# The input norm's root applied at the bank, and x split on arrival

## The reference, cut to what matters

```python
def rmsnorm(x, g):
    xf = x.astype(F32)
    y = xf * lax.rsqrt(jnp.mean(xf * xf, -1, keepdims=True) + EPS)
    return (y * g.astype(F32)).astype(x.dtype)

def mamba_layer(x, ...):
    h = rmsnorm(x, norm_g)
    proj = h @ w_in                  # z (4096), x/B/C (6144), dt (64)
    z, xbc, dt_raw = ...
    xbc, conv_new = causal_conv(xbc, conv_prev, conv_w, conv_b)   # per channel, 4 taps, silu
    dt = softplus(dt_raw + dt_bias)
    ...                              # recurrence over chunks, per head
    return x + y @ w_out, conv_new, s
```

## Time and profile before

| | us |
|---|---|
| median of 3 runs | 2285.92 |
| lowest, highest | 2285.22, 2286.48 |
| the profiled execution | 2281.53 |
| its span, first to last instruction | 2279.7 |
| TensorE busy | 2182.0 (96%) |
| VectorE busy | 1345.5 (59%) |
| ScalarE busy | 1109.9 (49%) |
| GpSimd busy | 1078.4 (47%) |

### The profile page before, as it was taken

One profiled execution on the slowest core, in us unless ns is written; L12 is line 12 of the kernel. 1 busy time (PEld: TensorE's weight loads), 2 busy tenths in 40 slices (PEclk: granted clock), 3 DMA queues, 4 the chain that ended last, 5 costly groups with the idle time before them and its releaser, 6 DMA issues. The chain is left out here.

```text
span 2279.7 us, 37485 instructions
## 1 busy us (share of the span) xinstructions
PE 2182.0 (96%) x13846; PEld 1868.0 (82%) x13846; DVE 1345.5 (59%) x2193; ACT 1109.9 (49%) x2824; POOL 1078.4 (47%) x712
## 2 busy tenths in 40 slices
PE   6999999999999999899998995999999999999799
PEld 5998888898998989598997773787787877877599
DVE  4766676767676767754214766665565665665510
ACT  4455454545545455553344544554554545545332
POOL 5665656565656655256672003533333333333166
PEclk9999999999999999899999997999999999999899
DMA  4564646564656465343443322212022122021544
GB/s 160 201 215 174 216 171 213 182 216 168 221 171 213 175 211 199 145 141 130 168 166 139 113 86 88 65 30 70 27 72 63 32 63 73 22 74 31 227 155 147
DMA packets 80623, 309.69 MB, mean 136 GB/s; under 512 B 14610, under 2 KB 22162, under 8 KB 54978
## 3 DMA queue, kind: packets, MB, share of 16 engines
q1 hardware_dynamic: 80450, 307.41, 39.1%
HBM read 279.72 MB, written 27.66 MB: 135 GB/s over the span
## 5 line engine op out<-in xcount | busy, mean ns | idle before, releaser
L691 POOL TENSOR_TENSOR w_lo<-raw,w_hi 128x1024 fp32r<-128x1024 f32 x218 | 540.2, 2499 | 367.9 <-ACT w_hi L903 367.8
L110 PE MATMUL bank<-h_hi,w_hi 128*128 128x304 f32 (+1 forms) x1520 | 471.7, 310 | 11.7 <-DVE h_lo L322 6.2
L112 PE MATMUL bank<-h_hi,w_lo 128*128 128x304 f32 (+1 forms) x1520 | 458.3, 302 | 0.0
L111 PE MATMUL bank<-h_lo,w_hi 128*128 128x304 f32 (+1 forms) x1520 | 456.5, 300 | 0.0
L903 ACT ACTIVATE w_hi<-raw 128x1024 fp32r<-128x1024 f32 x216 | 216.6, 1050 | 343.1 <-PE bank L112 334.8
L110 PE MATMUL bank<-b_hi,a_hi 128*128 128x512 f32 x896 | 357.7, 399 | 16.1 <-POOL a_lo L2442 8.5
L111 PE MATMUL bank<-b_lo,a_hi 128*128 128x512 f32 x896 | 350.8, 392 | 0.0
L112 PE MATMUL bank<-b_hi,a_lo 128*128 128x512 f32 x896 | 350.7, 391 | 0.0
L110 PEld LDWEIGHTS bank<-h_hi,w_hi 128*128 128x128 f32 x1520 | 286.1, 188 | 27.6 <-DVE h_lo L322 8.1
L111 PEld LDWEIGHTS bank<-h_lo,w_hi 128*128 128x128 f32 x1520 | 286.9, 189 | 2.3 <-issue 1.7
L112 PEld LDWEIGHTS bank<-h_hi,w_lo 128*128 128x128 f32 x1520 | 286.4, 188 | 0.0
(11 more groups left out here) (386 smaller groups left out, 4275.4 us busy)
## 6 DMA issues: line engine op xcount, KB each, us to landing
raw<-in_a_units SPq DMA_DIRECT2D x112, 1024.0 KB, 4.9
raw<-in_b_in_units SPq DMA_DIRECT2D x20, 1024.0 KB, 4.7
past<-in_cache SPq DMA_DIRECT2D x64, 288.0 KB, 3.2
pt<-in_cache_t SPq DMA_DIRECT2D x64, 256.0 KB, 2.5
raw<-in_o_units SPq DMA_DIRECT2D x16, 1024.0 KB, 5.2
s_in<-in_state_in SPq DMA_DIRECT2D x31, 512.0 KB, 7.0
out_state_out<-s_in SPq DMA_DIRECT2D x31, 512.0 KB, 6.9
s_t<-in_state_t SPq DMA_DIRECT2D x15, 1024.0 KB, 6.5
```

The lines of the kernel that those rows point to most:

```text
L110: nc.tensor.matmul(out, a[0], b[0], start=start, stop=False)
L111: nc.tensor.matmul(out, a[0], b[1], start=False, stop=False)
L112: return nc.tensor.matmul(out, a[1], b[0], start=False, stop=stop)
L691: nc.gpsimd.tensor_tensor(w_lo[u % 2][:, c], raw[u % 2][:, c], w_hi[u % 2][:, c].bitcast(F32), ALU.subtract).then_inc(lo_done, 1)
```

## The change

1. `load_stage` and `root_stage` are gone; a class `Entry` does their work inside `mamba_stage`. x arrives in quarters between the two halves of unit 0; `norms` goes out second; unit 1, `narrow`, `ones`, `eps` and ten small loads follow on the same queue.
2. x * norm (without the root) is split as it arrives: ScalarE makes the high part with norm as scale, VectorE the low part with one instruction. VectorE also makes the low parts of units 0 and 1, which GpSimd made, and clears the six buffers that GpSimd cleared.
3. The squares come behind the splits on ScalarE, into four free buffers; VectorE adds them up in five instructions, and one product by ones (halfway in the dt projection) gives the sum. ScalarE makes the root behind the split of unit 2.
4. The root is applied as a block leaves its bank: `evac` moves from ScalarE to VectorE and multiplies by `rs`. The old conv columns stay with ScalarE (`conv_past`), with a semaphore of their own. The dt rows are multiplied too (`rooted`).
5. In group 0 VectorE's order has the copies between the convs, `sums` and the copies of the turned rows (now `turned_back`) are apart, and ScalarE runs `ends` right behind `softplus`. From group 1 on, VectorE's copy of a block stands ahead of `heads` of the next iteration, and that of the tenth ahead of the first `add_out`.

The buffer `tmp` now shares its place with `y_lo`. The core of the diff:

```diff
     put("d_skip", [P, GROUPS, PAIRS])
     put("gate_norm", [P, GROUPS, PAIRS])
-    put("dt_bias", [HEADS, 1])
-    put("a_log", [HEADS, 1])
+    put("dt_in", [HEADS, 2])
+    put("rs", [P, TOK])
...
-def load_stage(nc, ctx, m, d):
...
-def root_stage(nc, ctx, m, psum, first, x_src, loads):
...
-class Scaled:
...
+class Entry:
+    SQUARES = ("gate0", "gate1", "y", "scratch")
...
+    def load(self, sp):
+        m, d = self.m, self.d
+
+        def x(n):
+            sp.dma_start(m["x"][:, 4 * n:4 * n + 4, :], d["x"][:, 4 * n:4 * n + 4, :]).then_inc(self.x_in[n], 16)
+
+        def first(n):
+            sp.dma_start(m["raw0"][:, HALVES[n]], d["a_units"][0][:, HALVES[n]]).then_inc(self.first_in[n], 16)
+        x(0)
+        sp.dma_start(m["norms"][:], d["norms"]).then_inc(self.gains_in, 16)
+        first(0)
+        x(1)
+        first(1)
+        x(2)
+        x(3)
+        sp.dma_start(m["raw1"][:], d["a_units"][1]).then_inc(self.second_in, 16)
+        sp.dma_start(m["narrow"][:], d["narrow"]).then_inc(self.narrow_in, 16)
+        for name in ("ones", "eps"):
+            sp.dma_start(m[name][:], d[name]).then_inc(self.ones_in, 16)
+        for dst, src in self.small:
+            sp.dma_start(dst, src).then_inc(self.small_in, 16)
+
+    def on_scalar(self, act):
+        nc, m = self.nc, self.m
+
+        def high(k):
+            if k % 4 == 0:
+                act.wait_ge(self.x_in[k // 4], 16)
+            nc.scalar.activation(m["h_hi"][:, k, :], m["x"][:, k, :], ACT.Copy, scale=self.gain(k)).then_inc(self.high_done, 1)
+
+        def first(n):
+            act.wait_ge(self.first_in[n], 16)
+            nc.scalar.activation(m["w_hi0"][:, HALVES[n]], m["raw0"][:, HALVES[n]], ACT.Copy).then_inc(self.first_high, 1)
+        nc.scalar.preload_act_table_set("natural_log_exp_and_others")
+        act.wait_ge(self.gains_in, 16)
         for k in range(KT):
+            high(k)
+            if k in (3, 7):
+                first(k // 4)
+        act.wait_ge(self.second_in, 16)
+        for c in HALVES:
+            nc.scalar.activation(m["w_hi1"][:, c], m["raw1"][:, c], ACT.Copy).then_inc(self.second_high, 1)
+
+    def squares(self, act):
         for k in range(KT):
+            self.nc.scalar.activation(self.m[self.SQUARES[k // 4]][:, k % 4, :], self.m["x"][:, k, :], ACT.Square).then_inc(self.squared, 1)
+
+    def root(self, act):
+        rs = self.m["rs"][:]
+        act.wait_ge(self.ones_in, 32)
+        act.wait_ge(self.summed, 1)
+        self.nc.scalar.activation(rs, self.SUM[:, 0:TOK], ACT.Ln, bias=self.m["eps"][:, 0:1], scale=1.0 / D_MODEL).then_inc(self.rooted, 1)
+        act.wait_ge(self.rooted, 1)
+        self.nc.scalar.activation(rs, rs, ACT.Exp, scale=-0.5).then_inc(self.rooted, 1)
+
+    def on_vector(self, dve, lo_done):
+        nc, m = self.nc, self.m
+        for name in ("dec0", "dec1", "cb", "c_diag", "cbuf0", "cbuf1"):
+            nc.vector.memset(m[name][:], 0.0)
+
+        def low(k):
+            dve.wait_ge(self.high_done, k + 1)
+            nc.vector.scalar_tensor_tensor(m["h_lo"][:, k, :], m["x"][:, k, :], self.gain(k), m["h_hi"][:, k, :].bitcast(F32),
+                                           op0=ALU.mult, op1=ALU.subtract).then_inc(self.low_done, 1)
+
+        def unit_low(u, n, high):
+            c = HALVES[n]
+            dve.wait_ge(high, n + 1)
+            return nc.vector.tensor_tensor(m[f"w_lo{u}"][:, c], m[f"raw{u}"][:, c], m[f"w_hi{u}"][:, c].bitcast(F32), ALU.subtract)
+        for k in range(KT):
+            low(k)
+            if k in (3, 7):
+                unit_low(0, k // 4, self.first_high).then_inc(self.first_low, 1)
+        for n in range(2):
+            unit_low(1, n, self.second_high).then_inc(lo_done, 1)
+
+    def add(self, dve):
+        nc, sq = self.nc, [self.m[n] for n in self.SQUARES]
+        v = Chain(dve, self.added)
+        for n in (1, 2, 3):
+            dve.wait_ge(self.squared, 4 * n + 4)
+            v(nc.vector.tensor_tensor(sq[0][:], sq[0][:], sq[n][:, 0:4, :], ALU.add))
+        v(nc.vector.tensor_tensor(sq[0][:, 0:2, :], sq[0][:, 0:2, :], sq[0][:, 2:4, :], ALU.add))
+        v(nc.vector.tensor_tensor(sq[0][:, 0, :], sq[0][:, 0, :], sq[0][:, 1, :], ALU.add))
+
+    def sum(self, pe):
+        pe.wait_ge(self.ones_in, 32)
+        pe.wait_ge(self.added, 5)
+        self.nc.tensor.matmul(self.SUM[:, 0:TOK], self.m["ones"][:], self.m["gate0"][:, 0, :], start=True, stop=True).then_inc(self.summed, 1)
 
...
-    def high(self, act):
+    def high(self, act, narrow_in):
+        act.wait_ge(narrow_in, 16)
         self.nc.scalar.activation(self.w_hi[:, 0:self.N], self.m["narrow"][:, 0:self.N], ACT.Copy).then_inc(self.split, 1)
-        self.nc.scalar.activation(self.seq_a, self.m["a_log"][:, 0:1], ACT.Exp).then_inc(self.a_step, 1)
+
+    def rates(self, act):
+        self.nc.scalar.activation(self.seq_a, self.m["dt_in"][:, 1:2], ACT.Exp).then_inc(self.a_step, 1)
+
+    def rooted(self, dve):
+        dve.wait_ge(self.proj, 1)
+        self.nc.vector.tensor_tensor(self.xb, self.P0[0:HEADS, 0:TOK], self.m["rs"][0:HEADS, :], ALU.mult).then_inc(self.scaled, 1)
 
     def softplus(self, act):
         nc, ab = self.nc, self.ab
-        act.wait_ge(self.proj, 1)
-        nc.scalar.activation(self.xb, self.P0[0:HEADS, 0:TOK], ACT.Identity, bias=self.m["dt_bias"][:, 0:1]).then_inc(self.a_step, 1)
+        act.wait_ge(self.scaled, 1)
+        nc.scalar.activation(self.xb, self.xb, ACT.Identity, bias=self.m["dt_in"][:, 0:1]).then_inc(self.a_step, 1)
...
+    def turned_back(self, dve):
+        nc = self.nc
...
-    def project(self, pe):
+    def project(self, pe, halfway):
         pe.wait_ge(self.split, 2)
         for k in range(KT):
+            if k == KT // 2:
+                halfway(pe)
...
-                if u >= 3:
+                if u == 2:
+                    sp.wait_ge(entry.first_low, 2)
+                else:
                     sp.wait_ge(lo_done, 2 * (u - 2))
...
+            entry.load(sp)
             unit(2)
...
-            scaled_x.on_pool(pool)
-            for u in range(1, LAST_UNIT + 2):
+            pool.wait_ge(lo_done, 2)
+            for u in range(2, LAST_UNIT + 2):
                 for n, c in enumerate(HALVES):
-                    if u == 1:
-                        first.high_done(pool, 1, n)
-                    else:
-                        pool.wait_ge(hi_done, 2 * (u - 2) + n + 1)
+                    pool.wait_ge(hi_done, 2 * (u - 2) + n + 1)
...
+                else:
+                    pe.wait_ge(entry.first_low, half + 1)
...
-                        scaled_x.low_done(pe, j)
+                        pe.wait_ge(entry.low_done, j + 1)
...
-                        steps.project(pe)
+                        steps.project(pe, entry.sum)
                     elif k == 3:
+                        entry.small_wait(pe)
                         steps.turn(pe)
...
-            def evac(kind, g, k):
...
+            def conv_past(kind, g, k):
+                if kind != "c":
+                    return
+                conv_saved.wait(act, g if k >= 2 else g - 1, k - 2 if k >= 2 else CONV_BLK - 2 + k)
+                if k == 0:
+                    act.wait_ge(co_in[g % 2], 16 * (g // 2 + 1))
+                nc.scalar.activation(by_seq(cbuf[k % 2], 7)[:, :, 0:3], conv_old[g % 2][:, k], ACT.Copy).then_inc(old_done.sem, 1)
...
-            scaled_x.on_scalar(act)
-            first.high(act, 1)
-            steps.high(act)
+            entry.on_scalar(act)
+            steps.high(act, entry.narrow_in)
+            entry.squares(act)
+            entry.small_wait(act)
+            steps.rates(act)
             for g in range(GROUPS):
                 u = unit_at(g)
                 first_in = IN_UNITS if g else CONV_BLK
                 of_g = blocks[at["z" if g else "c", g, 0]:][0:IN_UNITS]
                 for k in range(first_in):
                     split(u + k + 1)
+                    if g == 0 and k == 1:
+                        entry.root(act)
                     if k:
-                        evac(*of_g[k - 1])
+                        conv_past(*of_g[k - 1])
                     if g == 0 and k == 2:
                         steps.softplus(act)
-                    if g == 0 and k == 3:
                         steps.ends(act)
                     if k == 0 and g == 1:
-                        evac("z", 0, PAIRS - 1)
                         z_silu(0)
                     if g:
                         heads(g - 1, k)
                 for n in range(4):
                     split(u + first_in + n + 1)
-                    if n == 0 or g == 0:
-                        evac(*of_g[first_in + n - 1])
+                    if n == 0:
+                        conv_past(*of_g[first_in - 1])
                     start(g, n)
             last_heads()
...
+            def evac(kind, g, k):
+                block_wait(dve, kind, g, k)
+                src, rs = DENSE[at[kind, g, k] % 2], m["rs"]
```

(106 more changed lines are left out.)

64 lines of the change are left out of this document (21 added, 43 removed).

## The result

The changed kernel takes 2272.74 us (median; 2269.51 to 2273.84) against 2285.51 for the kernel before measured beside it: ratio 0.9945, interval 0.9933 to 0.9956, 12.8 us faster. The prediction was 2261.0 with 2252 to 2271: the sign holds, the gain is half of what was forecast, and the range missed by 1.7 us. The profiled execution of after took 2272.74 (span 2271.0), 8.7 us less span than the profiled one of before (which lay 4.0 us under its median). What lies behind the recurrence lasts between 1356.7 and 1364.9 us in the twelve profiles of this text, so I follow the gain by a mark inside the recurrence, the first row `e_cum<-e_raw` on ScalarE in each group.

What follows compares the result with a forecast made beforehand. TensorE was taken as the bound (busy 2182.0 of 2279.7 us), lacking at the entry and the seams. 18.5-1+7.5=25.0 us gain: 2256.5 for a run like the profiled one, 2261 as median, range 2252 to 2271 (8 in 10).

Steps and rivals of the forecast that it cites:

- Part 2: Evacuation on VectorE, 80 blocks: in-blocks cost zero, the seam's TensorE stall goes; gain 7.5 us, ends 0 to 8.5.
- Next late is `add_out` of block 1: Seam: this add, behind conv tap 0 (1.71 us), ends near 553.8; block 3 wants the bank near 554.3.
- a seam that is still there under another name: Seam of each group: listed as a sign that the forecast was wrong; no size given.
- rival B: Seam stays: `scaled`, `y_low` and the copy of c5 come late, cover only 0.6 us; gain 17.5, 2268 us; chance 0.12.
- Part 1: Entry: two barriers leave the path, so block c4 of group 0 starts at 51 instead of 69.51, 18.5 us earlier.
- the last two adds: Entry, sum of squares on VectorE: each waits out one GpSimd instruction; done at 30.5, free of it 26.0.
- The half-speed spell: Entry: TensorE's 3 us wait at the ones-product and a half-speed spell after it lie under the chain setting c4.
- a loss of 1: Group 0 behind c4's start: VectorE's copy c4 ends about 65, wanted at 64.8; 0 to 2 us lost, 1 taken.
- The in-blocks cost nothing: In-blocks: VectorE's copy is wanted 6.8 us or more later; cost zero, bounded above by 42 us.
- Rival C: In-blocks: VectorE's order becomes the bound, copies queued behind mixes and blocked convs; price 42 us, 2310; chance 0.05.
- D: Entry and seams: root eats the earlier start, c4 stays near 69, seams stay; 2286 us; chance 0.03.
- rival A: Entry: longer root chain, convs and adds blocked, loads late; c4 at 54 to 61, 2264 to 2271 us; chance 0.14.

Runs made afterwards that it cites:

- Quarters: The changed kernel with GpSimd's low part of each weight unit made in four instructions of 512 columns instead of two of 1024: 2258.82 us, ratio 0.9887.
- almost no GpSimd: The changed kernel with GpSimd subtracting only 64 of each 1024 columns from unit 4 on, other low parts left out: 2256.64 us, ratio 0.9874.
- the old kernel's control: The kernel before the change, with only GpSimd's low part cut into four 512-column instructions instead of two of 1024: 2283.28 us, ratio 1.0001.
- the doubled evacuations: The changed kernel with VectorE's copy out of the bank made twice in eight of ten in-blocks of groups 1 to 7: 2274.54 us, ratio 0.9956.
- the copies on ScalarE: The changed kernel with ScalarE copying in-blocks out of their banks in groups 1 to 7, the root left out there: 2269.84 us, ratio 0.9935.
- both edits of the entry's order: The changed kernel, separately, with ScalarE's root ahead of unit 2's split (2273.97 us), or VectorE's group 0 dt sums ahead of conv 1 (2270.93 us).
- eighths: The changed kernel with GpSimd's low part in eight instructions of 256 columns a unit: 2256.26 us, ratio 0.9882.
- the sums early: The changed kernel with GpSimd's 512-column instructions and, in group 0, VectorE's rooted and sums ahead of conv 1: 2253.51 us, ratio 0.9867.

## Why the prediction was wrong

**The step that failed is in Part 2**, "Next late is `add_out` of block 1": 7.5 us of gain became a loss of 1.9 (6 periods of 0.32, from the second mark to the last; half of it the slower out-blocks, which no step had). The old stall did go. I looked at one tap behind the seam, found half a microsecond of cover there, and stopped. That tap took 1.74, as its row said (1.71), and block 1's add was in time. The next tap took 2.20 and the copy of new conv columns 2.38, and the adds of later blocks came late. The trace of before shows these two shorter:

```profile
554.54 1.36 DVE L1077 SCALAR_TENSOR_TENSOR cacc<-cbuf,conv_w,cacc 128x328 f32<-128x328 f32 x1
...
558.35 0.17 DVE L1082 COPY conv_new<-cbuf 128x24 f32<-128x24 f32 x1
```

From 100 to 900 us this copy takes 0.18 at most in before, and 2.35 in the median in after. With the stall gone, the same orders meet GpSimd at other moments, so durations read beside the stall did not carry over. The right question was the rate: per out-block of 1.68 us VectorE owes one add of 0.47 and one tap, and a tap that is blocked by an instruction of 2.5 us does not fit. The last sentence of the prediction names this outcome ("a seam that is still there under another name"), and rival B allowed for it with a period unchanged; that the seam could make the period longer was in no case. Quarters (115.81), almost no GpSimd (115.81) and the old kernel's control (116.90) show the mechanism: the seam part is worth 1.1 us per group when no tap outlasts an out-block (1.68 at most with quarters). Lengths between 512 and 1024 columns were not tried.

**Part 1 was right in mechanism and 2 to 3 us too large**: c4 at 54.10 for 51, inside its own ends of 47 to 58 (52.97 and 53.19 in the two runs with the same entry, the doubled evacuations and the copies on ScalarE, where dense work started at 9.59 and 9.19). First, the loads: the first half of unit 0 reached ScalarE at 8.14 for 6.25, so dense work started at 10.51 for 8.7, and the third wide add ended at 26.6 for 24.7. Second, the last two adds were blocked as forecast (2.87 and 2.50), and the product behind the wait took 1.35 instead of 0.7, at a lower granted clock. The root was done at 34.6 for 32.3, and c4 follows it through conv 0, conv 1, `rooted`, the sums and `ends`, in the order written down. The memsets, 3014 columns by their rows and not the 3354 of the prediction, were over at 4.06 and cost nothing. The half-speed spell I had put "under the chain" (windows of after, same columns as above):

```profile
30.00:35.00 5.00, 2.82 (x9) 2.25 (x10) 2.31 (x3) 1.33 (x4) 1.71 (x1) 0.65 0.46 147
35.00:40.00 5.00, 5.00 (x27) 4.65 (x26) 4.89 (x4) 1.76 (x3) 4.23 (x2) 0.67 0.15 62
```

Granted clocks of 0.65 and 0.67 leave 27 matmuls in the second five microseconds instead of 38. It did lie under the chain almost to the end: when TensorE reached c4, GpSimd's low part was 0.84 us late, not the forecast 2.

**Behind c4** I took a loss of 1. The gain went from 15.4 at c4 to 13.2 at the first mark, a loss of 2.2: conv 2 took 7.79 us under two units of GpSimd back to back, and block c5 waited 1.61 for the copy of c3 behind it. The prediction had the loss one block later, at the copy of c4.

**The in-blocks cost nothing**, as forecast: no TensorE wait for an evacuation there in groups 1 to 7, and doubling most of them cost 0.43 per group. Rival C is out, and so is D. c4 at 54.10 just touches rival A (54 to 61), but A had the seam's stall gone for good, and so a larger gain.

**The tail** was in no step, and a cost of the change there is not shown. In this pair of profiles after lost 2.7 behind the last mark: three waits for `y` (3.4 together) where before had two (1.0), and a wait of 1.5 for `s_in` for 0.3. But the doubled evacuations and both edits of the entry's order leave the tail's code as it is in after, and there the same waits are 0.6 and 0.3. With quarters alone `s_in` is 3.3, with eighths or with the sums early 0.3. I take it to be the moment at which VectorE's last products meet GpSimd's last unit; no run was made to separate it.

The rule of the Trainium skill, SBUF — State Buffer, section "Who interferes with whom", that the loser of two engines blocks for the other's whole instruction, is borne out: the length of GpSimd's instruction, not its share of the time, set the price (pieces of 2520 ns: 2272.74 us; pieces of 1418 ns: 2258.82, with GpSimd busier by 60 us). The same section counts a copy among the instructions that can contend, under conditions on its operands, and here one of 24 columns did (2.38 us). The prediction applied the rule to the two adds at the entry and to the convs there, and not to the taps and copies of the seam.

## What to carry to other kernels

Where an engine's order feeds the bottleneck at a short beat, compare the beat (here 1.68 us per out-block) with the longest instruction that can block in that order, over the whole stretch and not only at its first place. When VectorE and GpSimd work beside each other on SBUF, cut GpSimd's instructions below that beat before giving VectorE more to do: it costs GpSimd time, which is free where nobody waits for it. Durations read in a trace hold for its own meeting of the two engines; a change that moves one of them by a microsecond can lengthen instructions that were never blocked before. And test a part again once the limit behind it has moved: the early sums were worth nothing with long GpSimd instructions and 5 us with short ones, and the quarters nothing without the change.

## What the runs showed of the hardware that was not expected

A copy of 24 columns that takes 0.17 us where GpSimd is idle takes 2.38 beside it: the wait does not shrink with the VectorE instruction. Halving GpSimd's subtraction does not halve it (2520 to 1418 ns, and 833 at a quarter of the width): by an estimate from these means 0.25 to 0.3 us of each is fixed, or is itself waiting. And 1.2 GHz came after short gaps: 2.98 us of waiting for the sum were followed by windows of 0.65 and 0.67, and a stretch with TensorE busy for 2.33 of 5 us by a window of 0.50.
